# Top-k by two token blocks and two heads, row fetches from the second tile of the down stage, gates from tile 26

## What is computed

```python
def block(xt):
    qry = (xt @ w_query).reshape(TOKEN_BLOCK, PEER_HEADS, 2, PEER_HALF)
    s1 = jnp.einsum('thd,hnd->thn', qry[:, :, 0], sub_keys1)      # 8 heads, 128 keys
    s2 = jnp.einsum('thd,hnd->thn', qry[:, :, 1], sub_keys2)
    v1, i1 = lax.top_k(s1, 16)
    v2, i2 = lax.top_k(s2, 16)
    cand = v1[..., :, None] + v2[..., None, :]                    # 256 candidates a head
    cand_idx = i1[..., :, None] * 128 + i2[..., None, :]
    top_s, pos = lax.top_k(cand, 16)
    idx = jnp.take_along_axis(cand_idx, pos, axis=-1)             # 16 of 16384 experts
    gate = jax.nn.softmax(top_s, axis=-1)
    pre = jnp.einsum('td,thkd->thk', xt, expert_down[idx])
    act = jax.nn.gelu(pre, approximate=False) * gate
    return jnp.einsum('thk,thkd->td', act, expert_up[idx])
```

## Time and profile before

| | |
|---|---|
| runs | 3889.01, 3889.85, 3898.88 us; median 3889.85 |
| profiled execution | 3899.26 us, span of its instructions 3897.4 us, mean granted clock 0.993 |
| PE busy | 3812.1 us (98%) |
| PEld busy | 3427.7 us (88%) |
| DVE busy | 2302.9 us (59%) |
| POOL busy | 1968.7 us (51%) |
| ACT busy | 1387.4 us (36%) |
| chain that ended last | PE 84%, DVE 10%, ACT 2% of the span |
| low half of an expert tile (L303, POOL) | 256 times, mean 4633 ns |
| high half of an expert tile (L623, ACT) | 256 times, mean 1912 ns |
| one gather (L311, POOL) | 128 down rows, mean 947 ns |
| one product of a row (L1124, DVE) | 128 times, mean 2283 ns |

### The profile page before, as it was taken

One profiled execution on the slowest core, in us unless ns is written; L12 is line 12 of the kernel. 1 busy time (PEld: TensorE's weight loads), 2 busy tenths in 40 slices (PEclk: granted clock), 3 DMA queues, 4 the chain that ended last, 5 costly groups with the idle time before them and its releaser, 6 DMA issues.

```text
span 3897.4 us, 51373 instructions
## 1 busy us (share of the span) xinstructions
PE 3812.1 (98%) x20037; PEld 3427.7 (88%) x20037; DVE 2302.9 (59%) x4061; ACT 1387.4 (36%) x1715; POOL 1968.7 (51%) x631
## 2 busy tenths in 40 slices
PE   7999999999999999999999999999999999999999
PEld 5676667777678878899999999999999999999999
DVE  5445455555568231699975656654156666666664
ACT  5333344444432223322233444443233333333332
POOL 2222322232234434466766556565566666666664
PEclk9999999999999999999999999999999999999999
DMA  3322222222233432257768878888778887888873
GB/s 141 126 92 78 83 75 83 78 78 78 78 132 140 166 114 87 87 221 285 307 248 308 310 292 313 312 298 315 283 280 299 307 301 297 303 305 298 299 296 130
DMA packets 175544, 811.06 MB, mean 208 GB/s; under 512 B 13568, under 2 KB 71168, under 8 KB 92544
## 3 DMA queue, kind: packets, MB, share of 16 engines
q1 hardware_dynamic: 59232, 399.47, 27.5%
q0 software_dynamic: 36864, 268.45, 18.6%
q10 hardware_dynamic: 79264, 140.56, 10.0%
HBM read 741.32 MB, written 72.35 MB: 209 GB/s over the span
## 4 chain that ended last, share of the span: by engine, by line
PE 84%; DVE 10%; ACT 2%; issue 2%; DVEq 1%; DMA 1%; ACTq 0%; POOL 0%
PE ps L1315 76%; PE ps L1534 2%; DVE psm L883 2%; PE ps L1397 2%; DVE expert_rows L1124 1%; DVE scores L887 1%; PE ps L1380 1%; PE ps L1389 1%; DVE s_all L1115 1%; PE ps L1331 1%; ACT w_hi L342 0%; DVE s_all L1113 0%; ACT scores L387 0%; PE ps L1480 0%; ACTq L723 0%
## 5 line engine op out<-in xcount | busy, mean ns | idle before, releaser
L303 POOL TENSOR_TENSOR w_e_lo<-w_e_raw,w_e_hi 128x2048 fp32r<-128x2048 f32 x256 | 1185.5, 4633 | 721.6 <-ACT w_e_hi L623 720.6
L296 POOL TENSOR_TENSOR w_lo<-w_raw,w_hi 128x2048 fp32r<-128x2048 f32 x115 | 540.0, 4696 | 1081.5 <-ACT w_hi L342 1081.5
L1315 PE MATMUL ps<-sn_hi,w_e_hi 128*128 128x384 f32 x2048 | 693.6, 339 | 9.6 <-POOL w_e_lo L303 9.6
L1315 PE MATMUL ps<-act_hi,w_e_hi 128*128 128x384 f32 x2048 | 685.2, 335 | 12.1 <-DVE h_dense L1235 12.1
L1315 PE MATMUL ps<-sn_lo,w_e_hi 128*128 128x384 f32 x2048 | 685.0, 334 | 0.0
L1315 PE MATMUL ps<-act_lo,w_e_hi 128*128 128x384 f32 x2048 | 685.0, 334 | 0.0
L1315 PE MATMUL ps<-act_hi,w_e_lo 128*128 128x384 f32 x2048 | 684.9, 334 | 0.0
L1315 PE MATMUL ps<-sn_hi,w_e_lo 128*128 128x384 f32 x2048 | 684.9, 334 | 0.0
L1235 DVE TENSOR_TENSOR h_dense<-ps,h_dense 128x384 f32<-128x384 f32 x512 | 284.7, 556 | 417.6 <-PE ps L1315 417.5
L623 ACT ACTIVATE w_e_hi<-w_e_raw 128x2048 fp32r<-128x2048 f32 x256 | 489.4, 1912 | 105.8 <-PE ps L1315 59.4
L1315 PE MATMUL ps<-xn_hi,w_hi 128*128 128x512 f32 x1088 | 448.2, 412 | 18.4 <-DVE xn_lo L797 18.4
(11 more groups left out here) (226 smaller groups left out, 5209.6 us busy)
## 6 DMA issues: line engine op xcount, KB each, us to landing
w_e_raw<-w_stream SPq DMA_DIRECT2D x256, 1024.0 KB, 7.6
w_raw<-w_stream SPq DMA_DIRECT2D x116, 1024.0 KB, 4.8
gel_dram<-gel_all ACTq DMA_DIRECT2D x32, 768.0 KB, 9.0
g_dram<-gate_buf ACTq DMA_DIRECT2D x12, 2048.0 KB, 13.5
gel_in<-gel_dram ACTq DMA_DIRECT2D x32, 768.0 KB, 4.5
g_exp<-g_dram ACTq DMA_DIRECT2D x32, 768.0 KB, 7.7
gate_dram<-g_raw ACTq DMA_DIRECT2D x32, 256.0 KB, 2.0
g_in<-gate_dram ACTq DMA_DIRECT2D x16, 512.0 KB, 6.0
```

What stands on the lines that cost most here:

```text
L296: nc.gpsimd.tensor_tensor(wlo[s][:, :], raw[s][:, :], whi[s][:, :].bitcast(F32), ALU.subtract).then_inc(lo_ready, 1)
L303: nc.gpsimd.tensor_tensor(e_lo[j % 4][:, :], e_raw[j % 4][:, :], e_hi[j % 3][:, :].bitcast(F32), ALU.subtract).then_inc(lo_ready, 1)
L1315: m = mm(ps[:, bank, 0:width], lhs[:, w], r, start=(n % (3 * per) == 0), stop=(n % (3 * per) == 3 * per - 1))
```

## The change

Top-k units take two token blocks and two heads (`lo`, `hi`, `pr`) instead of one block and four heads, so that unit `pr` waits for `sall` at 4 * pr + 4. Five units stand ahead of `scaled_lo` instead of two: blocks (2, 3) and (0, 1) with the first and the second pair of heads, and blocks (2, 3) with the third. The indices of the sparse block are made in two parts, the first 96 ahead of `scaled_lo`, the last 32 behind the pick of the fourth pair. GpSimd waits for them and for all of `scaled_lo` (the rows' slots lie in `h`) in loop step 1 instead of 6, and its gathers begin there. Three units are left for the down stage, with 20 products between them instead of 32. T_EXP, T_TURN and T_GATES go from 36, 38 and 41 to 20, 23 and 26; gates and products are spread at 6 in 5 tiles; T_ACT comes out at 112. The comparisons of `pick_of_heads` use `cand` as scratch instead of spent rows of `s_all`, and `idx3` lies elsewhere.

```diff
--- before.py
+++ after.py
@@ -44,12 +44,14 @@
 SLOTS = 4
 
 
-T_EXP = 36
-T_TURN = 38
-T_GATES = 41
-GATE_TILE = [T_GATES + 3 * n // 4 for n in range(N_GATES)]
-FIRST_ROWS = 36
-DOT_TILE = [T_GATES + 4 * j // 5 for j in range(PAIRS - FIRST_ROWS)]
+T_EXP = 20
+T_TURN = 23
+T_GATES = 26
+GATE_TILE = [T_GATES + 5 * n // 6 for n in range(N_GATES)]
+FIRST_ROWS = 24
+EARLY_PAIRS = 6 * TOPK
+FIRST_USED = [4, 9, 12, 14, 17, 20]
+DOT_TILE = [T_GATES + 5 * j // 6 for j in range(PAIRS - FIRST_ROWS)]
 T_ACT = DOT_TILE[-1] + 1
 ADD_TILE = list(range(T_ACT + 1, EXPERT_TILES - 3))
 ADD_TILE += [EXPERT_TILES + 1 + j for j in range(PAIRS - len(ADD_TILE))]
@@ -156,7 +158,7 @@
         rstd_h = at("rstd_h", 50, S)
 
         gel_all = [at("gel_all0", 191, 4 * TD), at("gel_all1", 141, 4 * TD)]
-        idx3, idx3_f, act3 = at("idx3", 197, PAIRS, U32), at("idx3_f", 197.5, PAIRS), at("act3", 198, PAIRS)
+        idx3, idx3_f, act3 = at("idx3", 206.75, PAIRS, U32), at("idx3_f", 207.25, PAIRS), at("act3", 198, PAIRS)
         i1_all, i2_all, tv_all = (at(n, 181 + 2 * k, S) for k, n in enumerate(["i1_all", "i2_all", "tv_all"]))
         cand = at("cand", 187, TT * 256)
         tk_v, tk_i, tk_if = at("tk_v", 203.5, 128), at("tk_i", 204, 128, U32), at("tk_if", 204.5, 128)
@@ -318,15 +320,17 @@
                 split(i)
             low(0)
             issued = 0
-            used_by = [9, 12, 15, 18, 21, 25, 28, 31, 34]
             for t in range(2 * EXPERT_TILES):
                 if t + 1 < 2 * EXPERT_TILES:
                     low(t + 1)
-                if t == 6:
+                if t == 1:
                     pool.wait_ge(idx3_ready, 1)
-                used = SLOTS * sum(u + 2 <= t for u in used_by) if t < T_GATES else FIRST_ROWS
+                    pool.wait_ge(slo_ready, CT)
+                used = SLOTS * sum(u + 1 <= t for u in FIRST_USED)
                 used += sum(u + 1 <= t for u in DOT_TILE) + sum(u + 1 <= t for u in ADD_TILE)
-                while t >= 6 and issued < min(used + SLOTS, 2 * PAIRS):
+                while t >= 1 and issued < min(used + SLOTS, 2 * PAIRS):
+                    if issued == EARLY_PAIRS:
+                        pool.wait_ge(idx3_ready, 2)
                     gather(issued)
                     issued += 1
 
@@ -1078,44 +1082,58 @@
                     vec.max_index(i_[:, 8:16], v_[:, 8:16], s_)
                 v.drain()
 
-            by_head = lambda t: t.rearrange("p (u c) -> p u c", u=4)
+            four = lambda t: t.rearrange("p (u c) -> p u c", u=4)
             grid = lambda t: t.rearrange("p u (a b) -> p u a b", a=TOPK)
             down_rows_of = lambda t: t.rearrange("p u (k o) -> p u k o", o=1).to_broadcast([P, 4, TOPK, TOPK])
             across = lambda t: t.rearrange("p u (o k) -> p u o k", o=1).to_broadcast([P, 4, TOPK, TOPK])
-            half_of = lambda t, half: by_head(t[:, :])[:, :, 16 * half:16 * half + 16]
+            half_of = lambda t, half: four(t[:, :])[:, :, 16 * half:16 * half + 16]
             sixteen = lambda t, n: [t[:, 16 * k:16 * k + 16] for k in range(n)]
             line16 = iota[:, 0:TOPK].rearrange("p (u a k) -> p u a k", u=1, a=1).to_broadcast([P, 4, TOPK, TOPK])
 
-            def top_of_heads(blk, four):
-
-                v.wait_ge(sall, 8 * four + 8)
-                first = 16 * KEYS * blk + 8 * KEYS * four
-                top16([s_all[:, first + KEYS * r:first + KEYS * r + KEYS] for r in range(8)],
-                      sixteen(tk_v, 8), sixteen(tk_i, 8))
+            def of_blocks(t, lo, hi, pr):
+
+                step = P * (hi - lo)
+                return t[:, P * lo:P * lo + 2 * step].rearrange("p (b c) -> p b c", b=2)[:, :, 32 * pr:32 * pr + 32]
+
+            def top_of_heads(lo, hi, pr):
+
+                v.wait_ge(sall, 4 * pr + 4)
+                rows_ = [16 * KEYS * blk + 2 * KEYS * (2 * pr + hd) + KEYS * half
+                         for blk in (lo, hi) for hd in range(2) for half in range(2)]
+                top16([s_all[:, r:r + KEYS] for r in rows_], sixteen(tk_v, 8), sixteen(tk_i, 8))
                 vec.tensor_copy(tk_if[:, :], tk_i[:, :])
-                vec.tensor_tensor(grid(by_head(cand[:, :])), down_rows_of(half_of(tk_v, 0)), across(half_of(tk_v, 1)), ALU.add)
-                v.drain()
-
-            def pick_of_heads(blk, four):
-
-                first = 16 * KEYS * blk + 8 * KEYS * four
+                vec.tensor_tensor(grid(four(cand[:, :])), down_rows_of(half_of(tk_v, 0)), across(half_of(tk_v, 1)), ALU.add)
+                v.drain()
+
+            def pick_of_heads(lo, hi, pr):
+
                 top16([cand[:, 256 * u:256 * u + 256] for u in range(4)], sixteen(top_v, 4), sixteen(top_p, 4))
-                slot = slice(P * blk + 64 * four, P * blk + 64 * four + 64)
-                vec.tensor_copy(tv_all[:, slot], top_v[:, :])
+                pairs = lambda t: t.rearrange("p (b c) -> p b c", b=2)
+                vec.tensor_copy(of_blocks(tv_all, lo, hi, pr), pairs(top_v[:, :]))
                 vec.tensor_single_scalar(top_a[:, :], top_p[:, :], 4, ALU.logical_shift_right)
                 vec.tensor_single_scalar(top_b[:, :], top_p[:, :], 15, ALU.bitwise_and)
                 v.drain()
                 vec.tensor_copy(top_f[:, 0:64], top_a[:, :])
                 vec.tensor_copy(top_f[:, 64:128], top_b[:, :])
                 v.drain()
-                spent = grid(by_head(s_all[:, first:first + 8 * KEYS]))
+                spent = grid(four(cand[:, :]))
                 for half, dst in ((0, i1_all), (1, i2_all)):
-                    vec.tensor_tensor(spent, down_rows_of(by_head(top_f[:, 64 * half:64 * half + 64])), line16, ALU.is_equal)
+                    vec.tensor_tensor(spent, down_rows_of(four(top_f[:, 64 * half:64 * half + 64])), line16, ALU.is_equal)
                     v.drain()
                     vec.tensor_tensor(spent, spent, across(half_of(tk_if, half)), ALU.mult)
                     v.drain()
-                    vec.reduce_sum(by_head(dst[:, slot]), spent, AX)
+                    vec.reduce_sum(of_blocks(dst, lo, hi, pr),
+                                   cand[:, :].rearrange("p (b u k) -> p b u k", b=2, k=TOPK), AX)
                     v.drain()
+
+            def sparse_indices(first, last):
+
+                part = slice(first, last)
+                vec.scalar_tensor_tensor(out=idx3_f[:, part], in0=i1_all[:, P * SPARSE + first:P * SPARSE + last],
+                                         scalar=float(KEYS), in1=i2_all[:, P * SPARSE + first:P * SPARSE + last],
+                                         op0=ALU.mult, op1=ALU.add)
+                v.drain()
+                vec.tensor_copy(idx3[:, part], idx3_f[:, part]).then_inc(idx3_ready, 1)
 
             def dot(j):
 
@@ -1137,27 +1155,33 @@
                                              op0=ALU.mult, op1=ALU.add).then_inc(row_used, 1)
 
             sparse = slice(P * SPARSE, P * SPARSE + P)
-            for blk in (SPARSE, 0):
-                top_of_heads(blk, 0)
-                pick_of_heads(blk, 0)
+            for pr in range(2):
+                for lo, hi in ((SPARSE - 1, SPARSE), (0, 1)):
+                    top_of_heads(lo, hi, pr)
+                    pick_of_heads(lo, hi, pr)
+            top_of_heads(SPARSE - 1, SPARSE, 2)
+            pick_of_heads(SPARSE - 1, SPARSE, 2)
+            sparse_indices(0, EARLY_PAIRS)
             for c in range(CT):
                 scaled_lo(c)
-            top_of_heads(SPARSE, 1)
-            pick_of_heads(SPARSE, 1)
-            vec.scalar_tensor_tensor(out=idx3_f[:, :], in0=i1_all[:, sparse], scalar=float(KEYS), in1=i2_all[:, sparse],
-                                     op0=ALU.mult, op1=ALU.add)
-            v.drain()
-            vec.tensor_copy(idx3[:, :], idx3_f[:, :]).then_inc(idx3_ready, 1)
-            top_of_heads(1, 0)
-            pick_of_heads(1, 0)
+            top_of_heads(SPARSE - 1, SPARSE, 3)
             v.wait_ge(turned, 1)
-            for k, (blk, four) in enumerate(((2, 0), (0, 1), (1, 1), (2, 1))):
-                for j in range(2 * SLOTS * k, 2 * SLOTS * k + SLOTS):
-                    dot(j)
-                top_of_heads(blk, four)
-                for j in range(2 * SLOTS * k + SLOTS, 2 * SLOTS * (k + 1)):
-                    dot(j)
-                pick_of_heads(blk, four)
+            for j in range(0, 4):
+                dot(j)
+            pick_of_heads(SPARSE - 1, SPARSE, 3)
+            sparse_indices(EARLY_PAIRS, PAIRS)
+            top_of_heads(0, 1, 2)
+            for j in range(4, 8):
+                dot(j)
+            pick_of_heads(0, 1, 2)
+            for j in range(8, 12):
+                dot(j)
+            top_of_heads(0, 1, 3)
+            for j in range(12, 16):
+                dot(j)
+            pick_of_heads(0, 1, 3)
+            for j in range(16, 20):
+                dot(j)
 
             per_head = lambda t: t[:, :].rearrange("p (u k) -> p u k", k=TOPK)
```

## The result

The changed kernel takes **3908.4 us** (median of 8 runs, 3906.1 to 3911.0), the kernel before, timed beside it, 3897.9 (8 runs, 3889.0 to 3899.3): ratio 1.0034, 95% interval 1.0023 to 1.0045. It is slower, and by more than 0.3% at the middle of the interval. The profiled execution took 3910.35 us, its span 3908.5: 11.1 more than the span of before.

The account below looks back on a forecast made before the run. TensorE's own work bounds the kernel; only its gaps can be won. Terms 14.8 + 6.6 - 10.0 = +11.4 gave 3910.7 against the profiled run; 3905.0 is the mean of 3901.3, 3910.1 and 3903.5; own range 3899 to 3912, overall 3893 to 3917.

Parts of the forecast that it names:

- the lower level: Faster timed runs of before, median 3889.9; guessed to lack tile 25's stall, which would put the changed kernel at 3910.1.
- First unit at 1504.6: Ahead of the down stage: the first top-k unit starts at 1504.6 us, once four score tiles are out.
- Rival (c): Ahead of the down stage: first unit does not begin with four score tiles; 11.8 us per period, 3917; chance 0.04.
- Five units, fifth at its end 1658.5; tile 0 at 1660.2, 14.8 late: Before the down stage: five units, lengthened by GpSimd's subtractions, delay scaled_lo and tile 0 by 14.8 us, bounds 0 and 17.
- Tile 0 takes 11.6: Down stage's first tile: 2.0 us wait for ScalarE goes, 2.4 us of clock after the stand cancels it.
- One stall at tile 20, 6.6: Head of down stage: weight half late behind gathers awaiting product 20; 4.9 us wait plus 1.7 clock, bounds 0 and 13.
- The new waits that I costed at nothing: Down stage: ScalarE at tile 20, TensorE's softmax at 23, GpSimd in step 1; each covered by 8 us or more.
- The rule weighed: Exclusive VectorE/GpSimd port lock would make tile 20's stall about 2 us; the sum used 4.9 from a 7.10 us copy.
- Stalls that go, 10.0: Head of down stage: weight-half waits of 1.2 at tile 19 and 7.1 at 25, plus 1.7 of clock, disappear.
- The join stays: Between down and up stages: the 12.1 us chain of last store, then gate load, is untouched and stays.
- (a): Rival, head of down stage: more stalls, tile 17 too and tile 20 longer; 3911 to 3918; chance 0.15.
- (b): Rival: shorter units; tile 0 on time 3879.9 (chance 0.05), or by half, 7 us late, 3887 to 3897 (chance 0.16).

Follow-up runs that it names:

- thin_comb: Changed kernel with GpSimd's subtraction ahead of the down stage cut to a quarter of its columns, the rest left out: 3852.3 us, ratio to before 0.9903.
- after_softmax_first: Also cited as 6: changed kernel with GpSimd's waits for late products moved later and products 20 to 23 put behind the softmax: 3901.2 us, ratio to before 1.0029.
- after: The changed kernel itself, against the kernel before: 3908.4 us, ratio 1.0034.
- 1: Changed kernel with GpSimd's waits for two products moved two and one loop steps later: 3908.0 us, ratio to before 1.0035.
- 2: Kernel before with GpSimd's waits for products moved one to two loop steps later: 3905.4 us, ratio to the unedited kernel before 1.0032.
- late_gates: Changed kernel with gates, softmax and first expert products put back where the kernel before has them: 3910.1 us, ratio to before 1.0039.
- comb_in_four: Changed kernel with each GpSimd subtraction ahead of the down stage done as four quarters back to back, nothing left out: 3873.2 us, ratio to before 0.9956.
- after_join: Changed kernel with the second gate group's load issued ahead of the waits for the down stage's last stores: 3906.1 us, ratio to before 1.0037.

## Why the prediction was right, point by point

**The total.** Forecast 3905.0 with 3899 to 3912 for its own case; measured 3908.4. The sum against the profiled execution said +11.4, 3910.7; it was +11.1, 3910.35. That the two agree so closely is in part luck: the term of tile 20 was 2.4 us too small and the join took 1.3 more, while the query stage ended 1.3 earlier, tile 0 was 0.5 shorter, the stall at tile 119 shrank by 0.9, and smaller pieces made up the rest. Against the lower level it said 3889.9 to 3910.1, a loss of 20; measured 19. This one is luck as far as is known, since the 20 rests on the guess that the lower level lacks the stall at tile 25, and no run supports that.

**First unit at 1504.6.** It was 1503.35, in an execution in which the query stage ended 1.3 us earlier. Rival (c) is out.

**Five units, fifth at its end 1658.5; tile 0 at 1660.2, 14.8 late.** The last indices follow at 1657.44, tile 0 starts at 1658.66, and TensorE stood 14.4 us. The length was forecast as 153.9 and was 154.1. Of the single meetings, those of the first two units came as laid out (1.28, 2.52 and 4.17 us). The 3 us at a comparison of the fourth unit and the 4 us in the fifth did not come (its copy took 0.33 us); in their place two stood in the fourth, 4.36 for the cast and 2.52 for the copy, 6.5 over their usual length. The sum held better than its pieces; thin_comb showed that its size, 12 us, is the meetings'.

**Tile 0 takes 11.6.** It took 11.11, at a granted 0.83. The clock cost 1.6 us instead of 2.4: in before the tile took 11.58, of which 2.04 were the wait for ScalarE, and 11.11 is 1.6 more than the other 9.54.

**One stall at tile 20, 6.6.** The place and the chain were right: product 20 ended at 1827.5 (1829.0 forecast), four gathers stood in GpSimd, the half of tile 20 was out at 1833.85 (1834.8), and tile 17 held, its half out at 1801.1 and due at 1802.9. The wait was 5.9 to 6.1 us instead of 4.9, since tile 20 was due at 1827.9 (1658.66 + 11.11 + 19 x 8.32) and not 1829.9: the query stage ended earlier and tile 0 was shorter, the product by only 1.5. The term of the clock was mis-sized: 1.7 was taken from tile 25, and tile 20 took 11.22 us at 0.73, 2.9 more than 8.3. Together 9.0 instead of 6.6, and after_softmax_first gave back 9.0. The new waits that I costed at nothing cost nothing: the shifted scores were out at 1828.5, the softmax at 1844.5, and TensorE waited for neither.

**The rule weighed.** By the rows above, the VectorE instructions that were long in the five units waited until the subtraction beside them ended (4.36, 4.17, 2.52 us), as the exclusive lock of the Trainium skill (SBUF — State Buffer, section "SBUF: two separate sides") has it, and quarters cut a single meeting to some 1.1 us. Between the scaled operand and tile 20 eight more were long, by 29 us in all, and none of them waited through more than one subtraction. So the size of the stall at tile 20 (5.9 us, where I had about 2 by the rule) does not speak against it. The multiplications of 9.76, 9.64 and 14.18 us beside two and three subtractions back to back do speak against it: one turn of GpSimd is not always the end of the wait. The measurements decide.

**Stalls that go, 10.0.** All went. The one at T_ACT + 5 shrank from some 1.2 us to 0.4 (6.3 less 5.9), where I had left it as it was.

**The join stays.** It stayed, with 12.9 us against 12.1, and 11.23 for the tile behind it against 10.70. The kernel before showed 13.4 in its second trace, and the versions with the join untouched 11.9 to 13.8: the 1.3 us lie within what the join varies by, and nothing ties them to the change.

**Rivals.** (a) did not come by a stall at tile 17, but the size of tile 20's went its way. (b) was ruled out by the comb: thin_comb brings its short units, and after does not have them.

**What I had wrong outside the sum.** The guess that the two levels of before are the stall at tile 25 found no support. And my first repair, to move GpSimd's waits, is not enough alone: the gathers are what feeds VectorE, and it only moved the wait (1, 2), until the products stood behind the softmax as well (6). I also had no term for the softmax's last multiplication meeting GpSimd's subtractions, which in after it happens to miss.

## What to carry to other kernels

When work is moved ahead in an in-order queue, look first at what stands behind it and has a date: five units ahead of one scaled operand cost 14.4 us, and with half a unit fewer tile 0 was on time. A wait that guards a ring of buffers is fed back, so putting it later delays the rows, the products and everything queued behind them; take the work without a date (products) out from ahead of the work with one (softmax) first. Look also at what one release starts on two engines at once: product 23 set off GpSimd's subtractions together with the softmax, and the softmax waited for them. If short VectorE instructions are longer on the mean than their kind, look at what GpSimd runs beside them, and if they are on the path, try cutting its long instructions.

## What the runs showed of the hardware

- **Some VectorE instructions and GpSimd's subtractions take turns by the instruction.** With the subtraction of 4.6 us done in quarters of 1.3 us (5.4 us for the four on the mean) the kernel is 35 us faster; 25.6 of them are TensorE's waits for the scores of the attention stages. Not every VectorE instruction takes part. Of those that began inside a subtraction of after from 1480 us on, with over 0.8 us of it left, all 12 CAST, COPY and TENSOR_TENSOR between SBUF tiles waited, and none of 72 MAX8, 76 FIND_INDEX8, 37 MATCH_REPLACE8 and 73 row products, which read PSUM.
- **Shorter turns don't shorten a long run of VectorE work.** In the one trace of it the five units lasted as long beside quarters (1622.63 - 1468.55 = 154.1 us) as beside whole subtractions (154.1): twelve short meetings in place of five long ones, several of them in a row, as next VectorE instruction met next quarter. That the sums are equal may be chance.
- **A turn can be passed over.** The softmax's multiplication of 0.69 us lasted 5.19 us beside one whole subtraction, 9.63 to 9.88 beside two with no gap between them (five traces), and 14.18 beside three. In all seven it is recorded as starting 0.12 to 0.14 us ahead of the first of them, and ends 0.5 to 0.6 us behind the last. A cast of 0.2 us lasted 4.22 beside the first of two that were 0.13 us apart, and got in between. What decides it no run here tells.
- **A load sent 9.0 us earlier, beside the last store, landed only 2.8 us earlier:** it took 15.22 us, where in after it takes 9.23 behind the store.
- **A stand of 6 us can cost as much clock as one of 13:** the tiles behind them took 11.22 and 11.23 us at a granted 0.73, that behind 7.1 us in before 10.06 at 0.83, and that behind 5.0 us in late_gates 10.02 at 0.83. Behind 5.4 us in comb_in_four it was 10.07, behind 5.6 in after_join 11.30.
